# The experts' blocks in one 512-column stream per half, with the down products of the block before behind it

## What is computed

```python
gate = p_group * top_p / jnp.sum(top_p, axis=-1, keepdims=True)
eid = gsel * EXPERTS_PER_GROUP + top_i
...
def expert_block(args):
    xb, e = args
    return (jax.nn.silu(xb @ w_gate[e]) * (xb @ w_up[e])) @ w_down[e]
```

## Time and profile before

| | |
|---|---|
| median of 3 runs | 3429.85 us |
| span of the profiled execution | 3433.8 us |
| TensorE busy | 3059.8 us (89%) |
| VectorE, ScalarE, POOL busy | 1553.3, 1115.5, 352.2 us |
| chain that ended last | TensorE's lines L1762, L1753 (twice) lead it |
| moved by DMA | 413.98 MB, mean 121 GB/s |

### The profile page before, as it was taken

How to read it: one execution, slowest core, us unless ns; L and a number is a source line. 1 busy time by engine, 2 the same in 40 slices (tenths; PEclk the granted TensorE clock), 3 DMA queues, 4 the chain that set the end, 5 groups by cost and what they waited for, 6 DMA issues and landing times. The chain is left out here.

```text
span 3433.8 us, 82115 instructions
## 1 busy us (share of the span) xinstructions
PE 3059.8 (89%) x33176; PEld 2305.5 (67%) x33177; DVE 1553.3 (45%) x3540; ACT 1115.5 (32%) x2626; POOL 352.2 (10%) x478
## 2 busy tenths in 40 slices
PE   5999999999968888879999959995399999999999
PEld 4777777777845555578888845553277777777776
DVE  3675666656657777623333337774011111111111
ACT  2343334333447777722222213432011111111111
POOL 0000000000000000000000000000422222222222
PEclk9999999999979999989999989997699999999999
DMA  5211121112130110011111144324577777767663
GB/s 209 65 59 56 52 66 57 57 49 70 57 100 7 48 47 9 9 60 42 42 42 42 41 178 147 135 98 149 75 282 280 283 279 276 283 231 262 218 243 112
DMA packets 211799, 413.98 MB, mean 121 GB/s; under 512 B 29738, under 2 KB 95530, under 8 KB 210016
## 3 DMA queue, kind: packets, MB, share of 16 engines
q1 hardware_dynamic: 191184, 360.07, 30.1%
q0 software_dynamic: 20368, 50.44, 4.2%
HBM read 334.97 MB, written 88.31 MB: 123 GB/s over the span
## 5 line engine op out<-in xcount | busy, mean ns | idle before, releaser
L287 PE MATMUL pj_big<-pj_xnT,pj_w_in 128*128 128x256 f32 x2816 | 646.1, 386 | 10.2 <-issue 8.8
L287 PEld LDWEIGHTS pj_big<-pj_xnT,pj_w_in 128*128 128x128 f32 x2816 | 545.8, 194 | 95.3 <-issue 16.3
L1753 PEld LDWEIGHTS ex_pg<-ex_wg,ex_xT 128*64 128x64 f32 x5120 | 292.1, 137 | 63.9 <-issue 61.2
L1753 PE MATMUL ex_pg<-ex_wg,ex_xT 128*64 128x128 f32 x5120 | 319.7, 275 | 6.8 <-issue 5.4
L1753 PE MATMUL ex_pu<-ex_wu,ex_xT 128*64 128x128 f32 x5120 | 312.9, 273 | 0.0
L1762 PE MATMUL ex_py<-ex_wd,ex_hT 128*64 128x512 f32 x1280 | 310.0, 603 | 1.7
L1753 PEld LDWEIGHTS ex_pu<-ex_wu,ex_xT 128*64 128x64 f32 x5120 | 291.3, 137 | 0.0
L1833 DVE TENSOR_TENSOR ex_hh<-ex_sg,ex_pu 128x128 f32<-128x128 f32 x160 | 46.0, 287 | 484.7 <-PE ex_pu L1753 484.7
L1202 PE MATMUL mg_po<-mg_w_out,mg_mix 128*128 128x512 f32 x512 | 230.2, 609 | 5.6 <-DVE mg_mix L1434 3.9
L708 ACT ACTIVATE at_e<-at_sc,at_nmx 128x512 f32<-128x512 f32 (+3 forms) x320 | 196.4, 620 | 115.2 <-DVE at_nmx L747 115.0
L1805 ACT ACTIVATE ex_sg<-ex_pg 128x128 f32<-128x128 f32 x160 | 44.3, 277 | 581.1 <-PE ex_pg L1753 581.1
(11 more groups left out here) (277 smaller groups left out, 4986.5 us busy)
## 6 DMA issues: line engine op xcount, KB each, us to landing
ex_wg<-in_w_exp_gate SPq DMA_DIRECT2D x32, 2048.0 KB
ex_wu<-in_w_exp_up SPq DMA_DIRECT2D x32, 2048.0 KB
ex_wd<-in_w_exp_down SPq DMA_DIRECT2D x32, 2048.0 KB
chunks_s<-pj_st SPq DMA_DIRECT2D x32, 642.0 KB, 4.0
rw_raw<-chunks_s SPq DMA_DIRECT2D x32, 642.0 KB, 3.9
pj_xt<-in_x SPq DMA_DIRECT2D x20, 512.0 KB, 3.7
qk_s<-pj_qo SPq DMA_DIRECT2D x64, 128.0 KB, 1.9
mg_xin<-in_x SPq DMA_DIRECT2D x8, 1024.0 KB, 6.1
```

What stands on the lines that cost most here:

```text
L287: ins = pe.matmul(out, lhs, rhs, start=(k == 0), stop=(k == KC - 1))
L1753: ins = pe.matmul(out[j * BT:(j + 1) * BT, 0:P], lhs, w[:, k, c0:c0 + P], start=(k == 0), stop=(k == KC - 1))
```

## The change

Every expert gets at least two blocks and the bound NB grows from 96 to 128, and the table with it. Gate and up weights share one tile, `wgu`, so that one matmul streams 256 columns of gate and 256 of up: 16 matmuls of 512 columns into one PSUM bank instead of 64 of 128. TensorE's body does, for block b: the two transpositions of h of block b-1 together, the four of x of block b+1, gate and up of block b, the down products of block b-1. The body that carries over into the next expert (`turn`) stands apart from the loop over an expert's other blocks (`rest`). Before the loops TensorE transposes x of blocks 0 and 1 and does gate and up of block 0; after them it finishes the last block. ScalarE and VectorE do silu and the product once on 256 columns, and one copy of hT. POOL gathers x two blocks ahead, in an order of its own, and copies an index more (`ida`). SP's refill waits for `s_pgu`.

```diff
-NB = 2 * S // BT + NE
+NB = 2 * S // BT + 2 * NE
...
-            chain(dve.tensor_scalar(nb[:, :], nb[:, :], 1.0, None, ALU.add))
+            chain(dve.tensor_scalar(nb[:, :], nb[:, :], 1.0, 1.0, ALU.max, ALU.add))
...
-        wg = [m.sb(f"wg{x}", [P, KC, DE]) for x in range(2)]
-        wu = [m.sb(f"wu{x}", [P, KC, DE]) for x in range(2)]
+        wgu = [m.sb(f"wgu{x}", [P, KC, 2, DE]) for x in range(2)]
...
-            for s0, b0, b1 in ((0, 0, 4), (1, 4, NB + 1)):
+            for s0, b0, b1 in ((0, 0, 4), (1, 4, NB + 2)):
...
                 n, first = blocks_of(sp, 4 * i + q - 2)
-                sp.wait_ge(s_pu, 2 * (first + n))
+                sp.wait_ge(s_pgu, first + n)
                 weights_in(sp, bass.ds(EPG * q + i, 1), q % 2)
                 sp.wait_ge(s_py, first + n)
...
+            def next_x(b):
+                pool.wait_ge(s_x, 16 * b + 32)
+                pool.sem_inc(s_apart, 1)
+                pool.tensor_copy(idx[:, :], tab[:, bass.ds(b + 2, 1), 0]).then_inc(s_idx, 1)
+                pool.wait_ge(s_idx, b + 3)
+                pool.sem_inc(s_apart, 1)
+                pool.wait_ge(s_px, b + 2)
+                pool.sem_inc(s_apart, 1)
+                gather_x()
+
+            def rows_acc(b, x):
+                pool.tensor_copy(ida[:, :], tab[:, bass.ds(b, 1), 0]).then_inc(s_ida, 1)
...
+            gather_x()
+            pool.wait_ge(s_x, 16)
+            pool.tensor_copy(idx[:, :], tab[:, 1:2, 0]).then_inc(s_idx, 1)
+            pool.wait_ge(s_idx, 2)
+            pool.wait_ge(s_px, 1)
+            gather_x()
             pool.wait_ge(s_tab[1], 32)
+            next_x(0)
+            rows_acc(0, 0)
+            next_x(1)
...
+                for x in range(2):
+                    b = 2 * i + 2 + x
+                    next_x(below(b, NB - 1))
+                    scatter(below(2 * i + x, NB - 2), x)
+                    pool.wait_ge(s_acc[1 - x], 16 * (i + x) + 16)
                     pool.sem_inc(s_apart, 1)
+                    rows_acc(below(b, NB - 1), x)
...
+            def gate_up(x):
                 for k in range(KC):
                     lhs = xT[:, k % 4, k // 4 * BT:(k // 4 + 1) * BT]
                     for j in range(2):
-                        c0 = 2 * P * j + P * part
-                        ins = pe.matmul(out[j * BT:(j + 1) * BT, 0:P], lhs, w[:, k, c0:c0 + P],
+                        ins = pe.matmul(pgu[j * BT:(j + 1) * BT, :, :], lhs, wgu[x][:, k, :, j * HE:(j + 1) * HE],
                                         start=(k == 0), stop=(k == KC - 1))
...
+            def body(b, x, before, i, y):
+
+                transpose_h(before)
                 pe.wait_ge(s_xT, b + 1)
...
                 pe.wait_ge(s_x, 16 * b + 32)
                 transpose_x()
...
+                gate_up(x)
+                down(before, i, y)
+
+            def rest(i, x, n, first):
+                with pe.Fori(0, n - 1) as j:
+                    body(below(first + j + 1, NB - 1), x, below(first + j, NB - 1), i, x)
+
+            def turn(i, x, n, first):
+
+                pe.wait_ge(s_wi[1 - x], 32 * (i + x) + 32)
+                pe.sem_inc(s_apart_pe, 1)
+                body(below(first + n, NB - 1), 1 - x, below(first + n - 1, NB - 1), i, x)
...
+            transpose_x()
+            pe.wait_ge(s_xT, 1)
+            pe.wait_ge(s_x, 32)
+            transpose_x()
+            pe.wait_ge(s_wi[0], 32)
+            gate_up(0)
+            with pe.Fori(0, NE // 2 - 1) as i:
                 for x in range(2):
                     n, first = blocks_of(pe, 2 * i + x)
+                    rest(i, x, n, first)
+                    turn(i, x, n, first)
...
+                    copy_h(b)
+                    silu(b + 1)
...
+            def gated(b):
+                dve.wait_ge(s_sg, b + 1)
+                dve.tensor_tensor(hh[:, :], sg[:, :], pgu[:, 1, :], ALU.mult).then_inc(s_hh, 1)
+                dve.wait_ge(s_px, b + 2)
+                copy_x()
...
                 for x in range(2):
+                    gated(2 * i + x + 1)
+                    add(below(2 * i + x, NB - 2), x, i)
```

More of the change, by code:

```diff
@@ L1613, in experts @@
         px = m.ps("px", [P, 4, P])
[L1614 to L1616 removed]
+        pgu = m.ps("pgu", [P, 2, HE])
+        phT = m.ps("phT", [P, 512])
         py = m.ps("py", [P, 512])
@@ L1621, in experts @@
         s_idx = m.sem("idx_done")
+        s_ida = m.sem("ida_done")
         s_idy = m.sem("idy_done")
@@ L1760, in down @@
[L1760 to L1766, removed]
-                pe.wait_ge(s_xT, b + 1)
[L1768 to L1773, removed]
+                ins.then_inc(s_pgu, 1)
@@ new lines, in transpose_h, with down @@
+            def transpose_h(b):
+                pe.wait_ge(s_hh, b + 1)
+                pe.wait_ge(s_hT, b + 1)
+                for part in range(2):
+                    ins = pe.transpose(phT[:, part * P:(part + 1) * P], hh[:, part * P:(part + 1) * P], ident[:, :])
+                ins.then_inc(s_phT, 1)
+            def down(b, i, x):
+                pe.wait_ge(s_wo[x], 16 * i + 16)
+                pe.wait_ge(s_yb, b + 1)
+                pe.wait_ge(s_hT, b + 2)
+                for part in range(2):
+                    for j in range(2):
+                        for n in range(2):
+                            ins = pe.matmul(py[n * BT:(n + 1) * BT, :], hT[:, part, j * BT:(j + 1) * BT],
+                                            wd[x][:, 2 * j + part, n * HD:(n + 1) * HD],
+                                            start=(part == 0 and j == 0), stop=(part == 1 and j == 1))
+                ins.then_inc(s_py, 1)
@@ L1789, in _, with silu, copy_h @@
             transpose_x()
[L1790 removed]
+            pe.wait_ge(s_xT, 1)
[4 more added lines that the diff above has]
+            with pe.Fori(0, NE // 2 - 1) as i:
                 for x in range(2):
                     n, first = blocks_of(pe, 2 * i + x)
[L1793 to L1796 removed]
+                    rest(i, x, n, first)
+                    turn(i, x, n, first)
+            i = NE // 2 - 1
+            n, first = blocks_of(pe, 2 * i)
+            rest(i, 0, n, first)
+            turn(i, 0, n, first)
+            n, first = blocks_of(pe, 2 * i + 1)
+            rest(i, 1, n, first)
+            last = below(first + n - 1, NB - 1)
+            transpose_h(last)
+            down(last, i, 1)
         @block.scalar
         def _(act):
[L1800 removed]
+            def silu(b):
+                act.wait_ge(s_pgu, b + 1)
+                act.activation(sg[:, :], pgu[:, 0, :], ACT.Silu).then_inc(s_sg, 1)
+            def copy_h(b):
+                act.wait_ge(s_phT, b + 1)
+                act.activation(hT[:, :, :], phT[:, 0:2 * P].rearrange("p (a n) -> p a n", n=P), ACT.Copy).then_inc(s_hT, 1)
+            act.sem_inc(s_hT, 1)
+            silu(0)
+            more = pairs(act)
+            with act.Fori(0, more) as i:
                 for n in range(2):
                     b = 2 * i + n
[L1803 to L1808 removed]
+                    copy_h(b)
+                    silu(b + 1)
+            copy_h(2 * more)
+            silu(2 * more + 1)
+            copy_h(2 * more + 1)
         @block.vector
```

109 lines of the change are left out of this document (30 added, 79 removed).

## The result

The changed kernel takes 3377.37 us (median of 4 runs, 3372.64 to 3380.47), the one before 3429.42 beside it (4 runs): ratio 0.9847, 95% interval 0.9833 to 0.9861, or -52.05 us. The forecast was 3402.9, so the direction was right and the gain twice as large, outside the range. The profiled execution has a span of 3378.5 us, 55.3 less than before.

The account below looks back on a forecast made before the run. TensorE's stream was taken to bound the experts' stage. Blocks shortened by 0.50 us gave -39.5, table +6.4, gather +4.3, filling +1.1, emptying +0.8: -26.9 us, to a median of 3402.9, range 3389 to 3416.

Parts of the forecast that it names:

- the jump back: TensorE's way to the next gate at every second expert: 0.52 us each, 0.10 a block, kept in the new block.
- the 0.62 for x: In each block, the x transpositions and the way back to the matmuls: 0.62 us, taken over into the new block.
- the drain: TensorE's step from half-array down products to a full-array transposition: 0.15 to 0.17 us, once per new block.
- the table: Start of the stage: long table loads growing from 93 to 126 blocks delay it by +6.4 us, bounds 0 and 8.
- nothing new is late: Chain behind gate_up: hh has 2.4 us slack, xT 2.7; POOL's three DMAs are issued before gate_up ends; cost nothing.
- Rivals 2 to 5: Boundaries cost more, 3427 (0.06); weights bind, 3419 (0.05); POOL holds VectorE, 3555 (0.04); halves not side by side, 3950 (0.01).
- rival 1: Larger gain: short stalls go wholly and the longer table's load costs little; 3394 us, chance 0.09.
- The emptying and filling: Ends of the pipeline: first h has no down in front, +1.1 us; last hT copy is bare, +0.8 us.
- The transposition in the middle of down: Second h transposition, no longer splitting the down products: 0.30 us of the clean block's 0.40 gain.
- 0.10 of the stalls as gone: Short stalls in the 128-column streams, 0.13 us a block: 0.10 goes with 32 instructions; bounds none or all.
- The second gather: Start: first gate_up waits for a gather issued after the first x transpositions, +4.8 us, net +4.3, bounds 2 and 7.
- rival (4): POOL's indirect DMAs hold VectorE between gate_up and the next transpositions; hh late 1.9 us a block, 3555 us, chance 0.04.

Follow-up runs that it names:

- e8: Changed kernel with the second h transposition moved behind gate_up, ahead of down, ScalarE's hT copy split: 3402.38 us, period 11.555 in every block.
- e17: Kernel before with only the second h transposition moved behind those of x, ahead of all down products; no software pipelining: 3384.41 us.
- e1: Changed kernel with gate and up again in 128 instructions of 128 columns per block: 3390.66 us, period 11.375 in every block.
- e13: Changed kernel with TensorE's wait for ScalarE's hT copy put right in front of gate_up: 3386.55 us, period 11.36 in every block.
- e11: Changed kernel with an added TensorE wait on the copy of x after eight down instructions: 3384.02 us.
- e3: Kernel before, old order, with gate and up of a half as one 256-column stream: 3413.80 us.
- e4: Kernel before with refills loading only the first row block of each weight array, so later experts use old weights: 3418.16 us.
- e10: Changed kernel with 128-column gate and up streams plus a TensorE wait on silu after four down instructions: 3381.56 us.
- e12: Changed kernel with 128-column gate and up streams plus a TensorE wait on the copy of x after eight down instructions: 3394.45 us.
- e14: Changed kernel with 128-column gate and up streams and TensorE's wait for the hT copy in front of gate_up: 3399.27 us.
- e5: Changed kernel with the table's constant back from 128 to 96 blocks: 3380.56 us.
- e9: Changed kernel with an added TensorE wait on silu after the first four down instructions: 3374.79 us.
- e6: Changed kernel with the long table loads held back until the first two gathers have landed: 3374.49 us, ratio 0.9864.
- e16: Changed kernel with long table loads held back and the second block gathered at once into its own buffer: 3367.85 us, ratio 0.9832.

## Why the prediction was right and wrong

The direction was right; the time missed the range because the block came out shorter than forecast: a mean period of 11.256 us for the 11.52 of the forecast, 20.4 us over the stage. No single term makes up that miss. The terms that failed are the jump back, which the forecast carried over unchanged, the 0.62 for x, the drain and the table.

- *TensorE's stream bounds the stage, blocks stay 80, nothing new is late.* Right. No wait on weights at a DMA share of 0.86; POOL is done 0.5 us ahead of gate_up's end, as counted; hh took 1.05 us behind the stream (1.0 forecast), xT 1.65 (1.75). Rivals 2 to 5 did not come. Of rival 1 both halves did (the stalls went wholly, the table cost little), but its 3394 was still 17 us too slow. The emptying and filling, +1.9 forecast, are 79 x 0.765 - 58.5 = 1.9.
- *The transposition in the middle of down is worth 0.30.* Right: e8 gives exactly 0.30 back, and e17's clean block falls by 0.41, of which 0.09 to 0.11 is the wait below. That the 128-column instructions gain little in themselves held too (0.12 measured by e1, 0.09 forecast). The Trainium skill (TensorE: Matmul & The Clock Gate, Back-to-back issue gap) gives a sustained 81 ns for 128 columns and 131 ns for 512, and about 56 and 216 ns for an isolated matmul. The streams here take 54.5 and 214 ns an instruction, near the second pair and far from the first.
- *"x and the way back 0.62."* Failed, by 0.09 a block, 7 us: I took an interval as work, and part of it was TensorE's wait for ScalarE's copy of hT, which the view doesn't show as idle time at that instruction. e13 measures it at 0.11.
- *"0.10 of it is the jump back at every second expert", kept unchanged in the new block.* This is the largest step that failed: 8 us, carried over without a reason. I took it for a property of the loop. It is one of the order: the last wait of the old body is met 2.2 us before the expert's end, where 2.9 and more cost nothing (e11 makes the jump by a late wait alone, e17 takes it away, e1 and e3 show that width has no part in it). That TensorE's sequencer can then not run ahead is my reading of it.
- *The drain, 0.15 to 0.17.* Mis-sized by 0.05 a block, 4 us: the forecast had 3.42 + 0.17 for down and the drain behind it, and 3.53 was measured. The 0.15 was read as 1.01 - 0.86, but four down instructions right behind a transposition also hold the 0.06 of entering; 0.10 is left, and e8 measures 0.10.
- *"I take 0.10 of the stalls as gone."* They went wholly, 2 us more. But my reason, that 128 instructions pass in 7 us, was wrong: in e1 they still pass and don't stall. Transfers take part (e4), and something of the old order; waits inside down (e10, e12) and in front of gate_up (e14) are not it. The wait and the signals inside the old streams were not tried by themselves, nor was the supply of instructions to TensorE: this stays open.
- *The table's 33 blocks, +6.4.* Mis-sized: 3.1 to 3.3 by e5, about 2 by the means of all traces. The 18.2 us are not in proportion to the blocks; a large fixed part lies in them. The second gather cost 3.9 for 4.8.
- *Nothing in the stages before.* The trace after starts this stage 3.7 us earlier with unchanged code; this is not a gain of the change.

Together 7 + 8 + 4 + 2 = 21, for the stage's 20.4 us; 4.2 come from the start and 3.7 from ahead of it.

## What to carry to other kernels

Before pricing a reordering of TensorE's stream, look where its last wait is met in each pass of the loop: one met shortly before a jump costs time at the jump, and one hidden in "the way to the next matmul" looks like work. Group full-array transpositions together; moving a single one gave four fifths of the gain. The software pipelining gave the rest only together with wider streams: it hides the activation chain, which a wider stream makes longer. And look at what is queued ahead of a stage's first operands: here loads in 8-byte pieces stood ahead of constants that were needed first.

## What was not expected of the hardware

- Two-instruction f32 matmuls hardly care for width: 16 pairs of 512 columns take 6.92 us, the same work as 64 pairs of 128 columns 7.04.
- Between the moment TensorE's last wait is met and the first matmul behind a jump back lie 2.3 to 2.75 us (e11 and the kernel before), while a wait met 2.9 us or more ahead is free (e8, e9, e17).
- The first indirect gather of the stage is slow even with the long table loads held back: in e6 it takes 9.3 us from issue (2443.66) to landing (2452.94), while the second in the changed kernel, issued at 2462.59, is used at 2465.95. It is not only the first: in e16 the second gather is issued at 2441.80, right behind the first, and TensorE, which waits for it, starts at 2449.75. What slows them was not tried.
- Short stalls of narrow streams sit at one place of the 128 instructions: in the kernel before all 82 late pairs are among pairs 40 to 48 of 64, in 54 of 78 blocks. They are 0.07 us of a block's average; the rest of the 0.13 lies where the streams begin and end.
- In the kernel before, VectorE's product of h starts 1.4 us (median) after the end of the up stream in the 75 cases in which an indirect DMA instruction of POOL lay in between, and 0.1 us after it in the other 81. In the changed kernel POOL was done 0.5 us before the stream's end, so nothing tested rival (4).
